# Order of the work inside a head pair: low-rank product ahead of the first T, convolution taps moved on VectorE, outputs regrouped, token-major v by 64x64 tiles

## What is computed

```python
def step(S, inp):
    r_t, w_t, k_t, v_t, kk_t, b_t = inp
    sa = jnp.einsum('bhij,bhj->bhi', S, kk_t)
    S = S * w_t[:, :, None, :] - sa[..., None] * b_t[:, :, None, :] + v_t[..., None] * k_t[:, :, None, :]
    return S, jnp.einsum('bhij,bhj->bhi', S, r_t)
...
# readout
mu = jnp.mean(y, axis=-1, keepdims=True)
var = jnp.mean(jnp.square(y - mu), axis=-1, keepdims=True)
yn = ((y - mu) * lax.rsqrt(var + LNX_EPS)).reshape(B, T, RWKV_DIM) * lnx_g + lnx_b
bonus = jnp.sum(r[:, :, None] * k_dir * r_k, axis=(2, 4))[..., None] * v
return ((yn + bonus.reshape(B, T, RWKV_DIM)) * g).astype(dtype)
```

## Time and profile before

| | us |
|---|---|
| median of three runs | 3150.03 |
| lowest and highest | 3148.62, 3157.8 |
| profiled execution, whole | 3148.07 |
| its span, first to last instruction | 3146.3 |
| busy: PE | 2962.2 |
| busy: DVE | 1744.2 |
| busy: ACT | 951.9 |
| busy: POOL | 436.0 |

### The profile page before, as it was taken

One profiled execution on the slowest core, in us unless ns is written; L12 is line 12 of the kernel. 1 busy time (PEld: TensorE's weight loads), 2 busy tenths in 40 slices (PEclk: granted clock), 3 DMA queues, 4 the chain that ended last, 5 costly groups with the idle time before them and its releaser, 6 DMA issues.

```text
span 3146.3 us, 70342 instructions
## 1 busy us (share of the span) xinstructions
PE 2962.2 (94%) x28320; PEld 2232.4 (71%) x28320; DVE 1744.2 (55%) x3292; ACT 951.9 (30%) x1635; POOL 436.0 (14%) x580
## 2 busy tenths in 40 slices
PE   5899999999999999999998899999989999999997
PEld 1345555555555555555555579999979999999997
DVE  1136555565455655556555354444358988886434
ACT  1122222222222222222222143333354444443333
POOL 0001110111101111011111020000003333331000
PEclk8899999999999999999999999999989999999999
DMA  8512222122121221212212254455434545554553
GB/s 330 234 72 100 88 75 88 57 99 93 70 88 62 94 90 73 88 62 95 88 48 97 108 208 159 177 185 187 161 134 174 185 176 185 184 177 162 180 174 137
DMA packets 66076, 412.32 MB, mean 131 GB/s; under 512 B 8176, under 2 KB 10864, under 8 KB 25328
## 3 DMA queue, kind: packets, MB, share of 16 engines
q1 hardware_dynamic: 65136, 407.51, 36.1%
q0 software_dynamic: 768, 2.10, 0.2%
HBM read 405.38 MB, written 4.19 MB: 130 GB/s over the span
## 4 chain that ended last, share of the span: by engine, by line
PE 85%; DVE 6%; DMA 3%; issue 3%; ACT 2%; POOL 0%; SPq 0%; ACTq 0%; DVEq 0%; POOLq 0%; PEldq 0%
PE PB L651 18%; PE Q L899 6%; PE Q L900 6%; PE Q L904 6%; PE PB L899 4%; PE PB L900 4%; PE PB L904 4%; PE CH L904 3%; PE CH L900 3%; PE CH L899 3%; DMA ring<-w_mod_dram 3%; PE Q L784 3%; PE PB L636 2%; PE Q L767 2%; PE CH L583 2%
## 5 line engine op out<-in xcount | busy, mean ns | idle before, releaser
L651 PE MATMUL PB<-hT,ring 128*128 128x512 f32 (+1 forms) x1536 | 687.9, 557 | 5.4 <-PEq L640 5.4
L1585 DVE TENSOR_TENSOR w_lo_r<-ring,w_hi_r 128x1536 fp32r<-128x1536 f32 (+3 forms) x178 | 387.6, 2177 | 270.3 <-ACT w_hi_r L1194 270.3
L1194 ACT ACTIVATE w_hi_r<-ring 128x2048 fp32r<-128x2048 f32 (+2 forms) x178 | 325.8, 1830 | 453.9 <-PE Q L904 211.8
L651 PEld LDWEIGHTS PB<-hT,ring 128*128 128x128 f32 x1536 | 252.4, 189 | 140.6 <-issue 96.9
L900 PE MATMUL PB<-hT_r,w_hi_r 128*128 128x256 f32 x832 | 204.5, 285 | 0.0
L1745 DVE TENSOR_TENSOR w_lo_r<-ring,w_hi_r 128x1408 fp32r<-128x1408 f32 x62 | 101.2, 1633 | 147.9 <-ACT w_hi_r L1308 147.9
L899 PE MATMUL PB<-hT_r,w_hi_r 128*128 128x256 f32 x704 | 175.7, 289 | 4.7 <-DVE hT_r L1672 4.7
L899 PE MATMUL Q<-ff_hi_r,w_hi_r 128*128 128x256 f32 x704 | 175.6, 288 | 1.8 <-ACT w_hi_r L1308 1.8
L900 PE MATMUL Q<-ff_lo_r,w_hi_r 128*128 128x256 f32 x704 | 172.9, 284 | 0.0
L899 PE MATMUL CH<-hT_r,w_hi_r 128*128 128x256 f32 x704 | 170.9, 283 | 0.0
L900 PE MATMUL CH<-hT_r,w_hi_r 128*128 128x256 f32 x704 | 170.9, 283 | 0.0
(11 more groups left out here) (262 smaller groups left out, 5991.0 us busy)
## 6 DMA issues: line engine op xcount, KB each, us to landing
ring<-w_mod_dram SPq DMA_DIRECT2D x96, 1024.0 KB, 5.2
ring<-w_up_dram SPq DMA_DIRECT2D x88, 1024.0 KB, 4.8
ring<-w_rkv_dram SPq DMA_DIRECT2D x48, 1024.0 KB, 4.8
ring<-w_down_dram SPq DMA_DIRECT2D x64, 704.0 KB, 4.0
ring<-w_ga_dram SPq DMA_DIRECT2D x16, 1024.0 KB, 4.8
ring<-w_gb_dram SPq DMA_DIRECT2D x16, 1024.0 KB, 4.7
ring<-w_pa_dram SPq DMA_DIRECT2D x16, 1024.0 KB, 4.8
ring<-w_out_dram SPq DMA_DIRECT2D x16, 1024.0 KB, 4.8
```

The costliest lines, as they stand in the source:

```text
L651: last = mm(PB[slot % 2][:, 0:cols], tile(n, kt), hT[:, kt, 0:cols], start=(kt == 0), stop=(kt == KT - 1))
L1194: f(w_hi_r[:, r % 2, 0:n], ring[:, r, 0:n], ACT.Copy).then_inc(hi_rdy, 1)
L1585: tt(w_lo_r[:, r, 0:n], ring[:, r, 0:n], as_f32(w_hi_r[:, r % 2, 0:n]), ALU.subtract).then_inc(lo_rdy, 1)
```

## The change

Five pieces, all inside a pair.

1. PE: the first small item, W0 of the next pair (in the last pair one part of the filler product), stands ahead of the first T instead of behind it. It is also ahead of the two waits of T, but behind the waits that stand ahead of all levels, that for the masked L rows among them.
2. DVE: the side taps of v of the next pair stand behind the last step of the scan instead of behind the last but one.
3. DVE: the parameter copy and the side taps of k of the pair after next stand behind the deviation instead of ahead of it.
4. PE: in the four output steps the products with VU of both directions come first and then those with the state of both; the accumulation groups, two in two banks, are open at the same time.
5. PE: the token-major copy of v contracts over the 64 channels of its own head instead of over 128 with zeros of the identity, with `small()` ahead of it.

```diff
                 pe.wait_ge(pb_free[V_ % 2], item_count(i, V_))
+                small()
                 for ch in range(NCH):
                     for h in range(2):
                         hr = slice(64 * h, 64 * h + 64)
-                        last = mm(CH[0][hr, ch * C:(ch + 1) * C], vx[:, ch * C:(ch + 1) * C], ident[:, hr],
+                        last = mm(CH[0][hr, ch * C:(ch + 1) * C], vx[hr, ch * C:(ch + 1) * C], ident[hr, hr],
                                   start=True, stop=True)
...
                 for lv in range(LEVELS - 1):
                     b = 2 << lv
+                    if lv == 0:
+                        if more >= 1:
+                            between(i + 1, 0)
+                        else:
+                            behind_last(0)
                     pe.wait_ge(zu_rdy, i * LEVELS + lv + 1)
                     pe.wait_ge(nlc_rdy, i * LEVELS + lv + 2)
...
-                    if more >= 1:
-                        between(i + 1, 3 * lv)
-                    else:
-                        behind_last(3 * lv)
-                    if more >= 1:
-                        between(i + 1, 3 * lv + 1)
-                    else:
-                        behind_last(3 * lv + 1)
+                    for k in range(3 * lv + (lv == 0), 3 * lv + 2):
+                        if more >= 1:
+                            between(i + 1, k)
+                        else:
+                            behind_last(k)
...
-                    for d in range(2):
-                        ch = chunk_at(d, s)
-                        if s >= 4:
+                    if s >= 4:
+                        for d in range(2):
+                            ch = chunk_at(d, s)
                             if s > 4:
                                 pe.wait_ge(y_sb[d], i * 4 + s - 4)
                             for h in range(2):
                                 rows = slice(64 * h, 64 * h + 64)
                                 mm(Q[2 * d][rows, 0:C], VU[d][:, ch, h], SC[d][h][:, ch, 1], start=True, stop=False)
+                        for d in range(2):
+                            ch = chunk_at(d, s)
                             for h in range(2):
...
-                    if more >= 1 and s == NCH - 2:
+                    if more >= 1 and s == NCH - 1:
                         outer(i + 1, 2, par_v)
...
                 tt(ra, yd[0], yd[1], ALU.add).then_inc(ysum_rdy, 1)
+                dve.wait_ge(mean_ps, i + 1)
+                stt(ra, Q[0][:, 0:T], -1.0 / HEAD, ra, ALU.mult, ALU.add).then_inc(dev_rdy, 1)
                 if more == 2:
                     fetch(par_vk, i + 2)
                     outer(i + 2, 0, par_vk)
-                dve.wait_ge(mean_ps, i + 1)
-                stt(ra, Q[0][:, 0:T], -1.0 / HEAD, ra, ALU.mult, ALU.add).then_inc(dev_rdy, 1)
```

## The result

The changed kernel takes 3079.64 us (median of four runs, 3072.86 to 3085.88) against 3150.61 us (four runs, 3148.62 to 3157.8) for the one before. The ratio is 0.9774, with a 95% interval of 0.9754 to 0.9794: 2.3% less. The profiled execution took 3077.41 us with a span of 3075.7 us, 70.6 us less than the span before. The forecast was 3085, in a range of 3074 to 3104.

A forecast was written before the change was run, and what follows sets the result against it. PE, busy 94% of the span, bounds the kernel, so only its idle time and clock can be won. 3.0 us in each of fourteen clean pairs, 47 us in all, plus 19 of clock gave 3085 us, range 3074 to 3104.

The forecast's parts named there:

- what would show it: Signs in the trace: full pairs of 93.5 us at clock 1.00, named gaps gone or left, outputs 0.24 us shorter.
- Part 1: W0 in PE's 1.77 us gap ahead of the first T: 0.43 us a pair, bounds 0 and 1.05.
- Part 2: v taps behind the last copies: PE's 1.23 us wait at the scan's last step goes, 0.05 deducted.
- Part 3: k taps behind the deviation: the variance product's 0.42 us wait goes; lower bound -0.2.
- Part 4: Outputs regrouped: two tile-shape changes of 0.12 us fewer in each of four steps, 0.96 us a pair.
- Part 5: Token-major v by 64x64 tiles: no effect on the 1.15 us group, bounds -0.1 and +0.1.
- rival (c): Token-major copies run in half the time by concurrent tiles: 9 us more gain, 3076 us; chance 0.04.
- The clock: Full pairs no longer drop to the lower level behind the gap ahead of T: about 19.3 us go.
- (a): Clock falls as before in the stretch around T: 3104 us if kept whole, 3094 by half; chance 0.20.
- (b): W0's gain eaten by the tanh, regrouping's by the state wait: 3106 us, one alone 3091 or 3100; chance 0.10.
- (d): Smaller gaps left behind T hold the clock low, slower than before: 3189 us; chance 0.02.
- The fifteenth pair: Pair without scan filler, waiting 2.28 us at its last step: 4 us gain expected.

The follow-up runs named there:

- regrouping alone: Kernel before with only the output products regrouped by tile shape; one execution, 3114.49 us.
- all but W0: Changed kernel with the low-rank product W0 back behind the first T; 3103.04 us, ratio 0.9854.
- split taps: Changed kernel with one side tap of v ahead of the last u copies and the other behind them; 3076.43 us, ratio 0.9765.
- one and two modulation products: Changed kernel, v taps split, first modulation product moved ahead of W0: 3068.44 us; second also moved, from third level to first: 3078.21 us.
- v taps alone: Kernel before with only the side taps of v moved behind the last step's copies; one execution, 3117.91 us.
- the kernel whose piece is worth nothing: Kernel before with only the token-major copy of v done by 64x64 tiles; one execution, 3144.13 us.
- W0 alone: Kernel before with only the low-rank product W0 moved ahead of the first T; 3122.11 us, ratio 0.9914.
- the unused product: Kernel before plus one 128x512 product, result unused, in the gap ahead of T, W0 in its old place; 3130.37 us, ratio 0.9936.

## Why the prediction was right

The time came out 5 us under the forecast, and all but one of the signs of "what would show it" are there: full pairs near 93.5 us at a clock of 1.00, a wait for the r taps ahead of A0, no gap at the last step or at the variance product, outputs in two groups. The gap of about 0.2 us between W0 and T is not. Step by step, for a clean pair, measured from starts on PE:

| step | forecast | alone | in the changed kernel |
|---|---|---|---|
| 1, W0 ahead of T | 0.43 | 0.39 | 0.39 |
| 2, v taps | 1.23 | 1.34 | 1.29 |
| r projection waits for v taps | -0.05 | | -0.17 (in step 4) |
| 3, k taps | 0.42 | 0.70 | 0.68 |
| 4, outputs | 0.96 | 1.17 | 0.88 |
| 5, token-major v | 0 | 0.00 | 0.00 |
| sum | 3.0 | 3.60 | 3.29 (sum of the rows 3.24) |

**Part 1 held**, with its reason: A0 starts late because of the r taps, and the 0.4 us survive to the last low-rank product, whose gap is 0.33 us now. One detail was off. T was to keep its 0.25 us behind POOL's copy; it starts at 549.01, 0.10 us behind 547.98 + 0.93 = 548.91. The squares' product did get a gap of 0.52 us, for the tanh, as was argued.

**Part 2 held.** The last step's wait is gone, and its worth was 0.06 to 0.11 us more than the gap shown.

**Part 3 was undersized.** The wait shown was 0.42 us, its removal brought 0.68 to 0.70. The product's later records account for 0.10 of the difference. The rest lies ahead of it: from the start of the last stretch of r projection to the product it was 542.30 - 540.42 = 1.88 us before and is 624.54 - 623.25 = 1.29 now, though only 0.42 was shown as idle. The direction was right and nothing was given back: the k taps fit in the cover, whose rest is the 0.50 us ahead of L1554 (2.20 us ahead of L1549 before).

**Part 4 was mis-sized twice, in opposite directions.** The first two output steps gave 0.30 and 0.29 us, not 0.24, since a change of tile shape costs 0.15 us, not 0.12. The third gave 0.17 (from L845's start to the next projection 533.72 - 532.02 = 1.70 before, 617.99 - 616.46 = 1.53 now): there the next step's small products follow directly, and they overlapped with the outputs already. The last gives 0.29 alone, but 0.12 in the changed kernel, where the v taps hold the projection back by 0.17; splitting the taps gave exactly that back. The prediction named this meeting and sized it at 0.05. That, and 0.13 us by which regrouping alone had shortened the gap that the v taps remove, make up the 0.31 us between 3.60 and 3.29: parts that act on the same wait do not add.

**Part 5 held.** Neither halving nor a penalty for both halves writing one bank: 1.15 us either way, 0.00 us a pair. The Trainium skill's "up to 2x" (TensorEngine Tiling (Array Packing), Theoretical Speedup) did not show for this shape, so rival (c) is out.

**The clock held, but its number is no second proof.** 19.3 us were expected to go and 19.6 went. Both are read against the same trace of the kernel before, so once no full pair falls the two have to agree but for what was miscounted. What was forecast, and came true, is that no full pair falls. The experiments show the cause: in six kernels with the long gap ahead of T the clock fell in three to eight of the fourteen full pairs, for an excess of 6.6 to 20.3 us, and each fall shows first in the low-rank products right behind T, which take 2.78 to 3.78 us there and 1.98 or 1.99 in all other pairs; in four with the gap filled, by W0 or by a product of no use, it fell in none and the excess is 0.7 to 0.9 us, and with a modulation product ahead of W0 it fell in none either. But the size of the loss does not follow from the gap: the single pieces that leave it in place as often lost 6.6 to 11.3 us. The prediction took the falls of its one trace as the cost, and it is luck that this execution (3148.07 us) was a usual one of its kernel (median 3150.03). It also counted seven of them; there are eight, the eighth in the pair of 100.09 us, behind a gap of 2.09 us. Rivals (a), (b) and (d) are out: parts 1 and 4 paid, and no full pair of the changed kernel is under 1.00, though gaps of 0.53, 0.53, 0.52 and 0.33 us stand there within 11 us.

**The fifteenth pair was oversized**: 4 us forecast, 2.24 measured. PE in the changed kernel at its first and at its last step:

```profile
1612.15 0.48 PE L838 MATMUL CH<-arena 64*64 64x64 f32 x8 [1.51 <-issue]
...
1636.21 0.33 PE L838 MATMUL CH<-arena 64*64 64x64 f32 x4 [0.20 <-DVE arena L1519]
1636.81 0.33 PE L838 MATMUL CH<-arena 64*64 64x64 f32 x4 [0.27 <-ACT arena L1157]
...
1639.74 0.33 PE L863 MATMUL Q<-arena 64*64 64x64 f32 x3 [1.32 <-issue]
```

The copy of direction 0 goes ahead, as the prediction says, and the 2.28 us of the earlier trace rows are gone. But direction 1's copy is ACT's, behind its centre tap, and then PE stands 1.32 us in the middle of the outputs, waiting for nothing that the trace shows ("issue"). A gap of that kind, 1.51 us, stands at the first step too, but that one is in the kernel before as well. The one at the end is new, and it comes with the moved v taps: in the fifteenth pair's last outputs the six kernels that have them there show 1.40 us (all but W0), 1.32 (the changed one), 1.05 (split taps), 0.80 and 0.53 (one and two modulation products) and 0.51 (v taps alone), and the other six show none. What it is stays open, and so does its share in the missing 1.76 us: this pair differs by more than that between traces (93.22 us in the kernel whose piece is worth nothing, 88.95 in the kernel before), and regrouping alone (85.77) and the v taps alone (86.02) each shortened it by more than the whole change did.

## What to carry to other kernels

Where PE is busy for over 90% of a stretch, look first at its longest idle gap and at the granted clock of the stretch behind it: a gap of about 2 us can cost more in speed than it does in idle time, and a product that fits in it can pay, here even a useless one. Move only work there whose operands have already come (a second modulation product gave all of the first one's gain back), and expect the next-latest input to take over part of what was won. Where two edits act on the same wait, price them together, since their single gains do not add.

## What the runs showed of the hardware

- **The lower clock follows a long gap, but not every time.** Behind gaps of 1.74 to 2.40 us ahead of small work, PE ran at its lower level of 1.2 GHz for a few us (3.41 us for work that takes 1.98): in three, three, four, six, seven and eight of fourteen pairs in six kernels whose gap is the same. Gaps of 1.96, 2.07, 2.08, 2.11 and 2.24 us stood in other pairs with no fall behind them, so the length of the gap alone does not decide. Behind the gap of 1.23 us at the last step it never did, in five kernels with fourteen such gaps each.
- **An idle gap costs more than the profile's idle time.** Removing 0.42 us gave 0.70, removing 1.23 gave 1.34. A product also starts sooner behind its releaser when PE has just been at work: 0.10 us behind POOL's copy instead of 0.25 (the traces of the changed kernel, of W0 alone and of the unused product agree on the 0.10).
- **A change of tile shape** between 128x64 and 64x64 costs about 0.15 us with groups of four records, worked out from this: in the steps where nothing overlaps, two fewer are worth 0.29 to 0.30 us.
- **64x64 and 128x64 fp32 tiles take the same time**: 1.15 us for 32 records of the token-major group either way.
